# Two heads' index scores in alternating halves of rows, and a last projection with tokens on partitions

## The reference, cut to what matters

```python
def sparse_mla_attention(q, c_kv, q_idx, k_idx, w_idx, w_uk, w_uv):   # per block of 128 queries
    s_idx = relu(einsum('btjd,bsd->btjs', q_idx, k_idx))               # 8 index heads j of 64, 512 keys s
    s_idx = einsum('btjs,btj->bts', s_idx, w_idx)                      # weighted sum over the heads
    _, idx = top_k(where(causal, s_idx, -inf), 128)
    ...                                                                # attention over the chosen keys
def hybrid_layer(x, ...):
    ...
    mixed = g_a * y_attn + g_r * y_rnn
    return x + mixed @ w_out                                           # the last projection
# the output: 0.5 * (mixed @ w_out) + x (the factor 2 of the gates is taken out), then rms_norm with the final gain
```

## Time and profile before

| | us |
|---|---|
| median of 3 runs | 1359.14 (1357.5 to 1359.92) |
| the profiled execution | 1360.57 |
| its span, first to last instruction | 1358.4 |
| TensorE busy | 1320.1 (97%) |
| DVE busy | 839.7 (62%) |
| ACT busy | 576.1 (42%) |
| mean granted TensorE clock | 0.991 |

### The profile page before, as it was taken

One profiled execution on the slowest core, in us unless ns is written; L12 is line 12 of the kernel. 1 busy time (PEld: TensorE's weight loads), 2 busy tenths in 40 slices (PEclk: granted clock), 3 DMA queues, 4 the chain that ended last, 5 costly groups with the idle time before them and its releaser, 6 DMA issues.

```text
span 1358.4 us, 16043 instructions
## 1 busy us (share of the span) xinstructions
PE 1320.1 (97%) x5982; PEld 1028.4 (76%) x5982; DVE 839.7 (62%) x1450; ACT 576.1 (42%) x871; POOL 216.9 (16%) x173
## 2 busy tenths in 40 slices
PE   7999988999999999999999999999999999999996
PEld 6777656888888888888888866687778866668885
DVE  6455753698888368837873463668887355552343
ACT  5344755644444133313432363314665246664221
POOL 1322211000000000000000022341004421123550
PEclk9999998999999999999999999999999999999999
DMA  5211110132222222232222231322122210002411
GB/s 196 93 62 63 37 57 31 62 111 106 93 93 93 94 93 95 102 113 93 93 93 93 94 125 62 114 104 93 62 93 93 94 62 32 32 32 93 155 63 62
DMA packets 17787, 116.51 MB, mean 86 GB/s; under 512 B 1984, under 2 KB 2240, under 8 KB 4544
## 3 DMA queue, kind: packets, MB, share of 16 engines
q1 hardware_dynamic: 16320, 108.35, 22.4%
q10 hardware_dynamic: 1408, 7.37, 1.5%
HBM read 111.52 MB, written 4.19 MB: 85 GB/s over the span
## 4 chain that ended last, share of the span: by engine, by line
PE 95%; DVE 2%; ACT 2%; DMA 1%; issue 0%; DVEq 0%; ACTq 0%; SPq 0%
PE PG L354 19%; PE PG L355 19%; PE PG L356 19%; PE PX L506 5%; PE PX L787 4%; PE PX L441 2%; PE PG L441 2%; PE PG L440 2%; PE PX L440 2%; PE PG L442 2%; PE PX L442 2%; PE PG L816 2%; PE PX L826 1%; PE PX L683 1%; PE PX L520 1%; PE PX L624 1%
## 5 line engine op out<-in xcount | busy, mean ns | idle before, releaser
L354 PE MATMUL PG<-XH,WH 128*128 128x512 f32 x992 | 393.1, 396 | 2.7 <-DVE XL L1595 2.7
L334 POOL TENSOR_TENSOR WL<-RAW,WH 128x512 fp32r<-128x512 f32 x160 | 213.7, 1367 | 1108.9 <-ACT WH L883 1108.9
L355 PE MATMUL PG<-XL,WH 128*128 128x512 f32 x992 | 386.2, 389 | 0.0
L356 PE MATMUL PG<-XH,WL 128*128 128x512 f32 x992 | 386.2, 389 | 0.0
L883 ACT ACTIVATE WH<-RAW 128x2048 fp32r<-128x2048 f32 x100 | 191.4, 1914 | 346.3 <-PE PG L356 234.4
L354 PEld LDWEIGHTS PG<-XH,WH 128*128 128x128 f32 x992 | 186.2, 188 | 48.9 <-issue 10.0
L355 PEld LDWEIGHTS PG<-XL,WH 128*128 128x128 f32 x992 | 186.3, 188 | 39.0 <-issue 1.9
L356 PEld LDWEIGHTS PG<-XH,WL 128*128 128x128 f32 x992 | 186.2, 188 | 38.8
L1332 DVE TENSOR_TENSOR WL<-RAW,WH 128x2048 fp32r<-128x2048 f32 x60 | 137.2, 2287 | 61.2 <-ACT WH L883 61.1
L1085 ACT ACTIVATE Z<-Z 128x512 f32<-128x512 f32 x32 | 20.3, 633 | 164.8 <-DVE Z L1646 164.8
L1630 DVE TENSOR_TENSOR U<-PG,R 128x1024 f32<-128x1024 f32 x32 | 39.1, 1223 | 51.5 <-PE PG L356 45.9
(11 more groups left out here) (311 smaller groups left out, 2029.8 us busy)
## 6 DMA issues: line engine op xcount, KB each, us to landing
RAW<-panels SPq DMA_DIRECT2D x100, 1024.0 KB, 4.7
x_spill<-XT ACTq DMA_DIRECT2D x1, 2048.0 KB, 7.1
XT<-x_spill ACTq DMA_DIRECT2D x1, 2048.0 KB, 7.9
outT<-SQ SPq DMA_DIRECT2D x4, 512.0 KB, 3.0
XT<-xT ACTq DMA_DIRECT2D x2, 512.0 KB, 6.6
XT<-xT SPq DMA_DIRECT2D x2, 512.0 KB, 9.2
RGW<-rgw ACTq DMA_DIRECT2D x1, 1024.0 KB, 4.7
UK<-uk ACTq DMA_DIRECT2D x1, 512.0 KB, 5.6
```

The lines of the kernel that those rows point to most:

```text
L334: ins = pool.tensor_tensor(WL[:, s].rearrange("p a b -> p (a b)")[:, piece], RAW[:, s, piece], WH[:, s].rearrange("p a b -> p (a b)")[:, p ...
L354: pe.matmul(o, WH[:, s, c, ms], xh[:, c, :], start=(c == 0), stop=False)
L355: pe.matmul(o, WH[:, s, c, ms], xl[:, c, :], start=False, stop=False)
L356: mm = pe.matmul(o, WL[:, s, c, ms], xh[:, c, :], start=False, stop=(c == DC - 1))
```

## The change

In words:
- `IDX_PLACES` has six places in each of the two panels, two groups apart. `idx_scores(v)` does two heads: for each of the three passes first the head on rows 0 to 63, then the one on rows 64 to 127, into two PX banks. From the third pair on it waits for the ReLUs of the pair before last. ACT and DVE still go unit by unit.
- "out2" is done with tokens on partitions: `last_panel(k)` does, for each of four token tiles, 12 matmuls (4 chunks of the contraction), two panels for columns 0 to 511 into PX, two for 512 to 1023 into PG. The host orders the weights for it.
- the residual is turned: `turn_x3(f)` does 16 transposes of 128x128 in the third (f = 0) and fourth (f = 1) panel of "ap", at its first quarter; ACT copies the four banks to X3T.
- DVE adds half the product to X3T; ACT squares and takes roots per token (as for "n4"), DVE makes the factor as a column and stores each tile's halves with it and the gain, which a new DMA of 128x1024 loads (FG). Eight DMAs of 256 KB write the output, not transposed.
- The matmuls that sum squares, `keep_warm` behind them, the logarithm and exponential with their table load, and the sums of pairs on DVE go.

```diff
-        IDX_PLACES = {3: {4 + n: n for n in range(12)}, 4: {2 + n: 12 + n for n in range(12)}}
+        IDX_PLACES = {3: {4 + 2 * n: n for n in range(6)}, 4: {2 + 2 * n: 6 + n for n in range(6)}}
+        OUT_ORDER = [(0, 0), (0, 1), (1, 0), (1, 1), (2, 0), (3, 0), (3, 1), (2, 1)]
@@ SP
-            for k in range(4):
-                sp.wait_ge(once("out_ready"), 2 * k + 2)
-                sp.dma_start(outT.rearrange("(c p) n -> p c n", p=P)[:, 2 * k:2 * k + 2, :], SQ2[:, 2 * k:2 * k + 2, :])\
-                    .then_inc(stored, 16)
-            sp.wait_ge(stored, 64)
+            for k, (t, f) in enumerate(OUT_ORDER):
+                sp.wait_ge(once("out_ready"), k + 1)
+                sp.dma_start(out[t * P:(t + 1) * P, f * S:(f + 1) * S], OT[:, t, f * S:(f + 1) * S]).then_inc(stored, 16)
+            sp.wait_ge(stored, 128)
@@ TensorE
-            def idx_scores(u):
-                qb, j = u // IDX_HEADS + 1, u % IDX_HEADS
+            def idx_scores(v):
+                qb, pair = v // 4 + 1, v % 4
                 n = (qb + 1) * P
-                rows = slice((j % 2) * HD, (j % 2) * HD + HD)
...
-                if u >= 4:
-                    pe.wait_ge(once("idx_relu"), u - 3)
-                qh, ql = (q[rows, j // 2, qb * P:(qb + 1) * P] for q in (QIH, QIL))
-                pe.matmul(PX[:, u % 4, 0:n], qh, KIH[rows, 0:n], start=True, stop=False)
-                pe.matmul(PX[:, u % 4, 0:n], qh, KIL[rows, 0:n], start=False, stop=False)
-                pe.matmul(PX[:, u % 4, 0:n], ql, KIH[rows, 0:n], start=False, stop=True).then_inc(once("idx_s"), 1)
+                if v >= 2:
+                    pe.wait_ge(once("idx_relu"), 2 * v - 2)
+                for k, (q, key) in enumerate(((QIH, KIH), (QIH, KIL), (QIL, KIH))):
+                    for m in range(2):
+                        rows = slice(m * HD, (m + 1) * HD)
+                        mm = pe.matmul(PX[:, (2 * v + m) % 4, 0:n], q[rows, pair, qb * P:(qb + 1) * P], key[rows, 0:n],
+                                       start=(k == 0), stop=(k == 2))
+                        if k == 2:
+                            mm.then_inc(once("idx_s"), 1)
-            gemm("ap", RH, OLO, ready=(once("o_split"), 0))
-            gemm_sums("out2", "n6", GA, ready=(once("m_split"), 0))
+            def turn_x3(f):
+                def turn():
+                    if f == 0:
+                        pe.wait_ge(reloaded, 16)
+                    else:
+                        pe.wait_ge(once("x3_copied"), NB)
+                    for t in range(NB):
+                        for c in range(4):
+                            mm = pe.transpose(PX[:, t, c * P:(c + 1) * P], XT[:, 4 * f + c, t * P:(t + 1) * P], IDN[:])
+                        mm.then_inc(once("x3_turned"), 1)
+                return turn
+            def last_panel(k):
+                p = FIRST["out2"][0] + k
+                f, half = divmod(k, 2)
+                pe.wait_ge(w_lo, p + 1)
+                if k < 2:
+                    pe.wait_ge(once("m_split"), 4 * k + 4)
+                if half == 0:
+                    if f == 0:
+                        pe.wait_ge(once("x3_copied"), 2 * NB)
+                    else:
+                        pe.wait_ge(evac, p - 2)
+                for t in range(NB):
+                    o = PG[:, t, :] if f else PX[:, t, :]
+                    ts = slice(t * P, (t + 1) * P)
+                    for c in range(4):
+                        wh, wl = (w[:, p % 2].rearrange("p a b -> p (a b)")[:, c * S:(c + 1) * S] for w in (WH, WL))
+                        xh, xl = (x[:, 4 * half + c, ts] for x in (XH, XL))
+                        pe.matmul(o, xh, wh, start=(half == 0 and c == 0), stop=False)
+                        pe.matmul(o, xl, wh, start=False, stop=False)
+                        mm = pe.matmul(o, xh, wl, start=False, stop=(half == 1 and c == 3))
+                    if half == 1 and t < NB - 1:
+                        mm.then_inc(once("dn_tile"), 1)
+                mm.then_inc(panel_done, 1)
+            p0 = FIRST["ap"][0]
+            for k in range(4):
+                one_panel(p0 + k, (p0 + k) % 2, RH, OLO, ready=(once("o_split"), 0) if k == 0 else None,
+                          quarter_done=turn_x3(k - 2) if k >= 2 else None)
+            for k in range(4):
+                last_panel(k)
@@ ACT
                 if t == 0:
                     act.dma_start(XT[:], spill).then_inc(reloaded, 16)
-            hi_squares("out2", "n6", GA, M2)
-            factor("n6", R[:])
+                if t in (1, 2):
+                    f = t - 1
+                    if t == 1:
+                        act.dma_start(FG[:], fin_in).then_inc(loaded_f, 16)
+                    for b in range(NB):
+                        act.wait_ge(once("x3_turned"), 4 * f + b + 1)
+                        act.activation(X3T[:, b, f * S:(f + 1) * S], PX[:, b, :], ACT.Copy).then_inc(once("x3_copied"), 1)
+            act.preload_act_table_set("sqrt_and_others")
+            p0 = FIRST["out2"][0]
+            hi_ahead(p0)
+            hi_ahead(p0 + 1)
+            for t in range(NB):
+                if t % 2 == 0:
+                    act.wait_ge(*((once("f_out"), 2) if t == 0 else (evac, p0 + 2)))
+                half_squares("n6", X3T, t, 0, M2)
+            token_factors("n6", X3T, (evac, p0 + 4), M2, p0 + 3)
@@ DVE
-                dve.tensor_scalar(DG[:, t, :], IDN[:], r[0], r[1], ALU.mult, ALU.mult).then_inc(once("tok_factor"), 1)
+                if norm == "n6":
+                    link(dve.tensor_tensor(r[2], r[0], r[1], ALU.mult))
+                else:
+                    dve.tensor_scalar(DG[:, t, :], IDN[:], r[0], r[1], ALU.mult, ALU.mult).then_inc(once("tok_factor"), 1)
...
+            dve.wait_ge(once("x3_copied"), 2 * NB)
+            for m in range(2):
+                ...
+                dst = X3T[:, 2 * m:2 * m + 2, 0:S]
+                dve.scalar_tensor_tensor(out=dst, in0=PX[:, 2 * m:2 * m + 2, :], scalar=0.5, in1=dst, op0=ALU.mult, op1=ALU.add)\
+                    .then_inc(evac if m else once("f_out"), 1 + m)
+            def store(t, f):
+                fs = slice(f * S, (f + 1) * S)
+                dve.scalar_tensor_tensor(out=OT[:, t, fs], in0=X3T[:, t, fs], scalar=RTK[:, 3 * t + 2:3 * t + 3],
+                                         in1=FG[:, fs], op0=ALU.mult, op1=ALU.mult).then_inc(once("out_ready"), 1)
+            for t in range(NB):
+                if t < 3:
+                    dve.wait_ge(once("dn_tile"), 28 + t)
+                else:
+                    dve.wait_ge(panel_done, p0 + 4)
+                dst = X3T[:, t, S:]
+                dve.scalar_tensor_tensor(out=dst, in0=PG[:, t, :], scalar=0.5, in1=dst, op0=ALU.mult, op1=ALU.add)\
+                    .then_inc(once("tok_y") if t < 3 else evac, 1 + t // 3)
+                if t == 1:
+                    first_half("n6")
+                    dve.wait_ge(loaded_f, 16)
+                if t in (1, 2):
+                    token_factor("n6", t - 1)
+                    store(t - 1, 0)
+                    store(t - 1, 1)
+            token_factor("n6", 2)
+            store(2, 0)
+            token_factor("n6", 3)
+            store(3, 0)
+            store(3, 1)
+            store(2, 1)
```

More of the change, by code:

```diff
@@ L82, in __call__, with build @@
         self.n = self.n + 1
-def build(nc, panels, xT, cols_in, lamv_in, wi_in, rgw_in, uk_in, uv_in, outT):
+def build(nc, panels, xT, cols_in, lamv_in, wi_in, rgw_in, uk_in, uv_in, fin_in, out):
     spill = nc.dram_tensor("x2_spill", (P, DC, S), F32, kind="Internal").ap()
@@ L171, in build @@
         NEC = at("NEC", [P, P], 204)
-        SQ2 = at("SQ2", [P, DC, S], 118)
+        X3T = at("X3T", [P, NB, 2 * S], 150)
+        OT = at("OT", [P, NB, 2 * S], 118)
+        FG = at("FG", [P, 2 * S], 134)
         COL = at("COL", [P, NCOLS], 196)
@@ L238, in build @@
         loaded_wi = sem("loaded_wi")
+        loaded_f = sem("loaded_f")
         spilled = sem("spilled")
@@ L899, in hi_stage @@
                     hi_ahead(p0 + n - 1)
-            def hi_squares(name, norm, dst, src):
-                p0 = FIRST[name][0]
-                for k in range(4):
-                    hi_ahead(p0 + k)
-                    if k == 3:
-                        act.activation(ES[:, 0:1], EPST, ACT.Ln)
-                    act.wait_ge(evac, p0 + k + 1)
-                    act.activation(dst[:, 2 * k:2 * k + 2, :], src[:, 2 * k:2 * k + 2, :], ACT.Square)\
-                        .then_inc(once(norm + "_sq"), 1)
             def factor(name, dst, bank=1, count=1):
-                if name != "n6":
-                    act.preload_act_table_set("natural_log")
+                act.preload_act_table_set("natural_log")
                 act.wait_ge(once(name + "_sum"), count)
@@ L1150, in _ @@
             for k in range(3, 7):
-                for u in IDX_PLACES.get(k, {}).values():
+                for u in [2 * v + m for v in IDX_PLACES.get(k, {}).values() for m in range(2)]:
```

(32 more changed lines are left out.)

19 lines of the change are left out of this document (6 added, 13 removed).

## The result

The changed kernel takes 1339.96 us in the median of 4 runs (1338.54 to 1343.95). The kernel before, beside it, takes 1358.32 us in the median of 4 (1356.85 to 1359.92). The ratio is 0.9869, 95% interval 0.9843 to 0.9896.

What follows compares the result with a forecast made beforehand. TensorE, 95% of the chain of waits, was taken as the bound. The terms -11.1 + 3.6 - 0.2 - 8.2 = -15.9 us gave 1344.7 from the profiled 1360.57, less 1.4 for the median: 1343.3 us, range 1341.0 to 1349.7.

Steps and rivals of the forecast that it cites:

- Bound: Whole span: TensorE is 95% of the chain of waits, so time goes mainly where TensorE gets less work.
- Pairs: Index panels: two heads on different row halves overlap and cost what one costs, 12 entries for 24; gain 11.1 us.
- the rival (halves in series): Index panels: the two heads' matmuls don't overlap in this number format; 6.2 us more, 1349.5 us; chance 8%.
- The loss of 0.6 to 0.9 us: Index panels: packed row tiles not quite free, 10 to 15% on the streams, making the gain 0.6 to 0.9 us smaller.
- ReLU and additions: Index panels: evacuation on ACT and DVE fits the 2.46 us period, no cost; rival that it bounds, 3 to 7 us, 4%.
- Turns: Attention projection, third and fourth panel: 32 residual transposes in two bursts on TensorE, without waits; 3.6 us lost.
- The rival in which the clock falls behind the bursts: Last six panels: TensorE's clock falls after the first transposes and stays down; 55 us more, 1398 us; chance 3%.
- Entry to the last projection: Second panel of the last projection: TensorE's wait for DVE's splits goes; gain 0.2 us.
- Tail: Last matmul's start to the end: 17.1 us becomes 8.9, gain 8.2 us; rival that it gives half, 1346.7 us, 5%.
- The last small product: Tail, DVE: the factor's last step becomes a product of two columns instead of a 128x128 diagonal, 0.2 us with its wait.
- the end behind the last store: Tail, from DVE's last store to the span's end: 2.5 to 3.4 us, taken nearer the first, with a 256 KB last DMA.
- its own range 1341.3 to 1345.5: Whole kernel: range of the main forecast, given 80%, from the tail's bounds and the transposes.

Runs made afterwards that it cites:

- same_half: The changed kernel with each entry's two heads on the same half of the rows, so their matmuls can't overlap; 1349.4 us, ratio 0.9935.
- head_major: The changed kernel with the loops of idx_scores exchanged, all three passes of one head, then all three of the other; 1339.03 us, ratio 0.9864.
- four_heads: The changed kernel with two pairs of heads in each index entry, six entries instead of twelve; 1337.68 us, ratio 0.9855.

## Why the prediction was right in its parts and missed its range

**Bound.** Right. What TensorE was spared, the span was spared, panel by panel.

**Pairs.** Right, -10.9 for -11.1. The pair costs what one head costs, at twice the column rate of the fp32 pair that I went by. From start to start an entry takes what it took: 0.55 us with 256 keys and 0.89 with 512, for one head and for two. The missing 0.2 us are 0.02 to 0.03 in each of 12 periods, in the panel's matmuls between the entries. `same_half` shows that the rival (halves in series) was sized right, 6.2 us, and didn't happen. The loss of 0.6 to 0.9 us that I had estimated from the Trainium skill, page TensorE: Matmul & The Clock Gate, section Measured speedup vs the span model, does not show: by these same entries a pair is within 0.01 us of a single head.

**ReLU and additions.** Right: DVE idles 0.93 us in each of the widest periods.

**Turns.** Right, +3.55 for +3.6, with no wait for the reload, for ACT's copies or for the next weights, and the clock at 1.00. The rival in which the clock falls behind the bursts is out.

**Entry to the last projection.** Right, -0.24 for -0.2.

**Tail.** Right to 0.2 us, -8.4 for -8.2, and right in each of its steps, since DVE's order sets them and nearly each had a row of the same instruction. The last small product (0.2 us) and the end behind the last store (2.5 us) had none and were estimates; they came out at 0.20 and 2.45.

**What failed is how the sum was turned into a time.** I wrote that the median of three runs is 1.4 us below the profiled one and set the sum against that median as if it were a fixed point, and gave the forecast "its own range 1341.3 to 1345.5" from the tail and the transposes. The attention's clock stood in the sum at nothing, and no reason was given for it. The earlier trace rows had it, at 0.89; I read it there only as a danger to another stage, and the rival made of it priced one fall that stays, 55 us. The runs show what the falls at the gaps are worth: up to five of some 1.6 us each. With them and up to 1.4 us at the start, one and the same kernel takes 1354.0 to 1360.8 before and 1338.4 to 1344.5 after. A median of four can fall almost anywhere in there, on both sides of the comparison, and that this one fell below the range was the luck of the draw. The first four of after had few falls (0.995, 0.996, 0.992, 0.996); the centre over 18 runs, 1341.8, is in the range, with 1343.3 near the runs at full count of falls. The profiled execution of before had all five, so the sum from it, 1360.57 - 15.9 = 1344.7, was the forecast for an execution with all five; after's seven at the lowest clock average 1343.9. A range of 1338 to 1346 for the likeliest case would have been honest. Why a fall comes behind a gap of 2.2 us in one execution and not in the next stays open.

## What to carry to other kernels

Price a step from the row of the same instruction in its neighbourhood, and let the engine that orders the tail set its times: that was good to 0.2 us in each of four parts here. Before giving a range, look whether a stretch has a granted clock below 1.00 behind idle gaps; count the gaps, price one, and put their number on both sides of the forecast, whether or not the change comes near them. To measure a small change in such a kernel, fill the gaps in both versions, or compare panel by panel in the traces: that cut the spread from 6 us to 1.5 here.

## What the runs showed of the hardware that I had not expected

Two row halves run beside each other whatever their program order, three matmuls deep (`head_major`). Going to 64 rows and back costs about 0.42 us per entry, whether it holds one head, two or four (0.40 and 0.42 in the earlier trace rows; 2.5 us for six entries fewer in `four_heads`). And the clock's answer to a gap is not a property of the gap: behind 2.22 us of idleness it fell to 1.2 GHz in one execution (mean 0.66 over the next 5 us) and stayed at 1.00 in the other.
